# An output stage that loads the first experts and gathers the first blocks before it ends

## What is computed

```
x  = x + g1 * (concat(gla, attn) @ w_out)
h2 = modulate(rms_norm(x), shift2, scale2)
scores = sigmoid(h2 @ router_w); top 4 of 8 groups, top 8 of 64 experts; weights normed * 2.5
routed = sum over the 8: w_e * (silu(h2 @ wg[e]) * (h2 @ wu[e])) @ wd[e]      (FF = 128)
shared = (silu(h2 @ swg) * (h2 @ swu)) @ swd                                  (FF = 256)
y  = rms_norm(x + g2 * (routed + shared))
```

## Time and profile before

| | us |
|---|---|
| median of 3 runs (lowest, highest) | 1642.26 (1637.18, 1643.11) |
| profiled execution, device time | 1637.02 |
| its span, first to last instruction | 1635.2 |
| PE busy | 1496.2 (91%) |
| DVE busy | 722.9 (44%) |
| POOL busy | 564.6 (35%) |
| ACT busy | 530.4 (32%) |
| mean granted PE clock | 0.956 |

### The profile page before, as it was taken

How to read it: one execution, slowest core, us unless ns; L and a number is a source line. 1 busy time by engine, 2 the same in 40 slices (tenths; PEclk the granted TensorE clock), 3 DMA queues, 4 the chain that set the end, 5 groups by cost and what they waited for, 6 DMA issues and landing times. The chain is left out here.

```text
span 1635.2 us, 28990 instructions
## 1 busy us (share of the span) xinstructions
PE 1496.2 (91%) x9223; PEld 922.0 (56%) x9224; DVE 722.9 (44%) x1453; ACT 530.4 (32%) x1255; POOL 564.6 (35%) x615
## 2 busy tenths in 40 slices
PE   5999999999899999999999599999999999999645
PEld 2654678787757774555465255555455555555312
DVE  2300144442455652787843244444344444444238
ACT  2400165443156651211100133333333333333212
POOL 0001134344253211111254255555455555444322
PEclk8999999999989999999999799999999999999868
DMA  9991002100183017012000699999999999986487
GB/s 340 343 341 39 20 2 52 47 14 17 64 305 131 27 63 297 26 52 90 1 0 0 240 315 335 337 331 339 345 342 328 336 295 303 274 206 120 64 314 286
DMA packets 108677, 301.66 MB, mean 184 GB/s; under 512 B 13020, under 2 KB 24112, under 8 KB 107836
## 3 DMA queue, kind: packets, MB, share of 16 engines
q1 hardware_dynamic: 81390, 212.09, 34.5%
q0 software_dynamic: 25920, 83.91, 21.3%
q10 hardware_dynamic: 1296, 4.72, 0.7%
HBM read 230.26 MB, written 80.90 MB: 190 GB/s over the span
## 5 line engine op out<-in xcount | busy, mean ns | idle before, releaser
L2103 PE MATMUL ps_g<-w_exp,mix 128*64 x1408 | 327.4, 386 | 5.8 <-DVE own_gu L2198 2.8
L2106 PE MATMUL ps_g<-own_gu,mix 128*64 128x256 f32 x1408 | 327.4, 386 | 0.0
L2103 PEld LDWEIGHTS ps_g<-w_exp,mix 128*64 128x64 f32 x1408 | 187.7, 138 | 108.2 <-issue 11.9
L2052 POOL DMA_INDIRECT sum_rows<-mix,scatter_row x66 | 128.6, 1948 | 173.1 <-DVE mix L2141 147.1
L2106 PEld LDWEIGHTS ps_g<-own_gu,mix 128*64 128x64 f32 x1408 | 187.7, 138 | 0.0
L2075 PE MATMUL ps_y<-w_exp,hidT 128*64 x352 | 171.6, 610 | 6.3 <-ACT own_d L2154 6.3
L2076 PE MATMUL ps_y<-own_d,hidT 128*64 128x512 f32 x352 | 171.6, 610 | 0.0
L511 PE MATMUL ps_f<-late,hT 128*128 128x256 f32 x624 | 144.9, 389 | 0.0
L2198 DVE COPY own_gu<-w_exp 128x2048 f32 x89 | 109.5, 1231 | 59.2 <-issue 46.4
L511 PEld LDWEIGHTS ps_f<-late,hT 128*128 128x128 f32 x624 | 119.9, 195 | 18.7 <-issue 1.9
L1480 PE MATMUL ps_o<-wo,mixT 128*128 128x512 f32 x288 | 126.0, 596 | 0.5 <-DVE h L1726 0.5
(11 more groups left out here) (328 smaller groups left out, 2497.6 us busy)
## 6 DMA issues: line engine op xcount, KB each, us to landing
w_exp<-in_exp_w_gate SPq DMA_DIRECT2D x64, 512.0 KB, 7.6
w_exp<-in_exp_w_up SPq DMA_DIRECT2D x64, 512.0 KB, 14.6
w_exp<-in_exp_w_down SPq DMA_DIRECT2D x64, 512.0 KB, 21.4
sum_rows<-mix SPq DMA_DIRECT2D x10, 2048.0 KB, 18.4
sums<-sum_rows SPq DMA_DIRECT2D x36, 512.0 KB, 15.1
ada_ring<-in_w_ada SPq DMA_DIRECT2D x8, 2048.0 KB, 11.1
wring<-in_w_ada SPq DMA_DIRECT2D x3, 2048.0 KB, 13.1
h_rows<-h SPq DMA_DIRECT2D x9, 512.0 KB, 2.6
```

The costliest lines, as they stand in the source:

```text
L2052: pool.indirect_dma_start(out=dram["y"][k % 2], out_offset=bass.IndirectOffsetOnAxis(ap=si[k][:], axis=0), in_=y[k], in_offset=None, bound ...
L2103: pe.matmul(ps_g[par][0:HALF, 0:2 * FF].rearrange("p (k f) -> p k f", k=2), xT[par][:, j * P:j * P + HALF], w[:, bass.ds(slot * 3, 2), ff] ...
L2106: last = pe.matmul(ps_g[par][HALF:P, 0:2 * FF].rearrange("p (k f) -> p k f", k=2), xT[par][:, j * P + HALF:(j + 1) * P], own_gu[par][:, :, ...
```

## The change

- `w_exp` (the ring of eight slots) is allocated around both stages. In the output stage its first 36 KB are `h2T` (slots of experts 0 to 2), and `w_out`, the rows of modulation and one of the two `mixT` tiles lie behind it.
- When all of `gate_up` is done (`h2T` is read for the last time) SP loads experts 0, 1 and 2 and waits for them at the stage's end.
- POOL, after the table is written, gathers blocks 0, 1 and 2 into the last three rows of `keep["mix"]` (the x and y buffers change places), then makes the addition of tile 7 and waits for the gathers.
- `down(8)` writes `ps_h` instead of `ps_o`, so it waits for `eb_kept` (block experts copied out of that bank) and no longer for `keep_shared(7)`. DVE makes the last tile's addition to `x1` itself.
- `write_table` copies the gates last instead of first.
- `experts` issues expert 3 at once, posts experts 0 to 2 as ready without a wait, issues 4 to 6 after blocks 0 to 2 are multiplied (`gu_done` 1 to 3), and gathers block 3 first. Before it issued 3 to 6 after `gu_done` 1 to 4.

```diff
@@ -1337,11 +1339,14 @@
             return nc.alloc_semaphore(name)
         GE = 8
-        wo = sb("wo", [P, KD, D])
+        wf = keep["w"][:].rearrange("p s n -> p (s n)")
+        wof = wf[:, KD * T:KD * (T + D)]
+        wo = wof.rearrange("p (j n) -> p j n", n=D)
         rw = sb("rw", [P, KD, NE])
-        mixT = [sb(f"mixT{i}", [P, KD, P]) for i in range(2)]
+        mixT = [wf[:, KD * (T + D) + 6 * D:].rearrange("p (j t) -> p j t", t=P), sb("mixT1", [P, KD, P])[:]]
         g2rows = keep["g2"]
-        rows = sb("rows", [P, 3, 2, D])
+        rof = wf[:, KD * (T + D):KD * (T + D) + 6 * D]
+        rows = rof.rearrange("p (w c n) -> p w c n", w=3, c=2)
         h2 = [sb(f"h2_{i}", [P, D]) for i in range(2)]
         ssq = sb("ssq2", [P, NT])
         lnm = sb("lnm2", [P, NT])
...
@@ -1385,14 +1389,13 @@
         pairs = sb("r_pairs", [1, NE], I32)
         lastf = sb("r_lastf", [1, 3])
-        wof = wo[:].rearrange("p j n -> p (j n)")
         place = [wof[:, i * 1024:(i + 1) * 1024].rearrange("p (k r) -> p k r", r=P) for i in range(2)]
         entry = [wof[:, 2048 + i * 2048:2048 + i * 2048 + 2 * TOPK * TAB].rearrange("p (k v b) -> p k v b", v=2, b=TAB) for i in range(2)]
         empty = wof[:, 6144:6144 + TAB]
         s_sh, h_sh, hT_sh = ([wof[:, 6400 + (2 * k + i) * FS:6400 + (2 * k + i + 1) * FS] for i in range(2)] for k in range(3))
         wgu = keep["mix"][:, 0:2 * KD * FS].rearrange("p (k n) -> p k n", k=2)
         wd = keep["mix"][:, 2 * KD * FS:2 * KD * FS + 2 * D].rearrange("p (k n) -> p k n", k=2)
-        t6 = [mixT[i][:].rearrange("p j n -> p (j n)") for i in range(2)]
+        t6 = [mixT[i].rearrange("p j n -> p (j n)") for i in range(2)]
         ps_t = ps("ps_t4", [P, 2, 512])
         ps_o = ps("ps_o4", [P, 2, 512])
...
@@ -1454,8 +1464,13 @@
                     sp.dma_start(wgu[:, 0, :], dram["sh_w_gate"].rearrange("(p j) f -> p (j f)", j=KD)).then_inc(wgu_in, 16)
                     sp.dma_start(wgu[:, 1, :], dram["sh_w_up"].rearrange("(p j) f -> p (j f)", j=KD)).then_inc(wgu_in, 16)
                     sp.dma_start(wd, dram["sh_w_down"].rearrange("(k p) n -> p k n", p=P)).then_inc(wd_in, 16)
+            sp.wait_ge(gu_done, NT)
+            for e in range(W_EARLY):
+                for k, w in enumerate(expert_weights(dram)):
+                    sp.dma_start(keep["w"][:, 3 * e + k, :], w[e, :, :]).then_inc(first_w, 16)
             sp.wait_ge(h2_out[0], 16 * 5)
             sp.wait_ge(h2_out[1], 16 * 4)
+            sp.wait_ge(first_w, 48 * W_EARLY)
         @block.tensor
         def _(pe):
...
@@ -1532,12 +1547,14 @@
                 if t == 0:
                     pe.wait_ge(wd_in, 16)
                     pe.wait_ge(gx_done, NT)
+                elif t < NT - 1:
+
+                    pe.wait_ge(t_done, t)
                 else:
-
-                    pe.wait_ge(t_done, t)
+                    pe.wait_ge(eb_kept, 1)
                 for q in range(2):
                     for k in range(2):
-                        last = pe.matmul(ps_o[:, q, :], hT_sh[t % 2][:, k * P:(k + 1) * P],
+                        last = pe.matmul(down_bank(t)[:, q, :], hT_sh[t % 2][:, k * P:(k + 1) * P],
                                          wd[:, k, q * 512:(q + 1) * 512], start=(k == 0), stop=(k == 1))
                 last.then_inc(down_done, 1)
...
@@ -1680,6 +1697,13 @@
                 pool.tensor_tensor(v[:, :, 0, :], v[:, :, 0, :], tokp1[:, t:t + 1].unsqueeze(2).to_broadcast([P, TOPK, TAB]),
                                    ALU.mult).then_inc(entry_done, 1)
+            def gather(k):
+                pool.tensor_copy(keep["gi"][k][:], keep["tab"][:, k, 0:1]).then_inc(gi_made, 1)
+                pool.wait_ge(gi_made, k + 1)
+                pool.indirect_dma_start(out=keep["mix"][:, (6 + k) * D:(7 + k) * D], out_offset=None, in_=dram["h2"],
+                                        in_offset=bass.IndirectOffsetOnAxis(ap=keep["gi"][k][:], axis=0),
+                                        bounds_check=T - 1, oob_is_err=False).then_inc(first_x, 16)
+
             def add_shared(t):
                 pool.wait_ge(t_done, t + 1)
                 pool.tensor_tensor(keep["x1"][:, t, :], keep["x1"][:, t, :], t6[t % 2], ALU.add).then_inc(x_done, 1)
...
@@ -1694,8 +1718,15 @@
                 if t % 2:
                     add_shared(t // 2 + 1)
             entries(NT - 1)
-            for t in range(NT // 2 + 1, NT):
-                add_shared(t)
+            add_shared(NT - 4)
+            add_shared(NT - 3)
+            pool.wait_ge(tab_written, 1)
+            pool.wait_ge(h2_out[0], 16 * 5)
+            pool.wait_ge(h2_out[1], 16 * 4)
+            for k in range(X_EARLY):
+                gather(k)
+            add_shared(NT - 2)
+            pool.wait_ge(first_x, 16 * X_EARLY)
         @block.vector
         def _(dve):
...
@@ -1797,7 +1828,7 @@
                     dve.wait_ge(rows_in[3], 16)
                 if t >= 2:
                     dve.wait_ge(x_done, t - 1)
-                dve.tensor_tensor(t6[t % 2], ps_o[:].rearrange("p n k -> p (n k)"), keep["g2"][:, cond_of(t), :], ALU.mult).then_inc(t_done, 1)
+                dve.tensor_tensor(t6[t % 2], down_bank(t)[:].rearrange("p n k -> p (n k)"), keep["g2"][:, cond_of(t), :], ALU.mult).then_inc(t_done, 1)
             def slots():
...
@@ -1849,18 +1880,18 @@
             def keep_block_experts():
                 dve.wait_ge(eb_turned, 1)
-                dve.tensor_copy(keep["bexp"][:].rearrange("o (p c) -> o c p", c=2), ps_e)
+                dve.tensor_copy(keep["bexp"][:].rearrange("o (p c) -> o c p", c=2), ps_e).then_inc(eb_kept, 1)
             def write_table():
                 tab = keep["tab"]
                 dve.wait_ge(tab_done, NT)
                 token = ps_tab[:, 0, :]
-                dve.tensor_copy(tab[:, :, 2].bitcast(F32), ps_tab[:, 1, :])
                 step(dve.tensor_scalar(empty, token, 0.0, float(NOWHERE), ALU.is_equal, ALU.mult))
                 step(dve.scalar_tensor_tensor(out=tab[:, :, 0], in0=empty, scalar=-1.0, in1=token, op0=ALU.add, op1=ALU.add))
                 step(dve.tensor_scalar(empty, token, 0.0, spare, ALU.is_equal, ALU.mult))
                 step(dve.scalar_tensor_tensor(out=tab[:, :, 1], in0=empty, scalar=shift, in1=token, op0=ALU.add, op1=ALU.add))
+                dve.tensor_copy(tab[:, :, 2].bitcast(F32), ps_tab[:, 1, :]).then_inc(tab_written, 1)
             mix_half(0)
             for t in range(NT):
...
@@ -1899,6 +1930,15 @@
             write_table()
             keep_shared(NT - 2)
             keep_shared(NT - 1)
+            dve.wait_ge(t_done, NT)
+            dve.tensor_tensor(keep["x1"][:, NT - 1, :], keep["x1"][:, NT - 1, :], t6[(NT - 1) % 2], ALU.add)
+
+
+def expert_weights(dram):
+
+    return (dram["exp_w_gate"].rearrange("(e p j) f -> e p (j f)", p=P, j=KD),
+            dram["exp_w_up"].rearrange("(e p j) f -> e p (j f)", p=P, j=KD),
+            dram["exp_w_down"].rearrange("(e p) n -> e p n", p=P))
 def experts(nc, dram, keep):
...
@@ -1918,15 +1958,14 @@
         def sem(name):
             return nc.alloc_semaphore(name)
-        NW = 8
         AHEAD = 4
         FOURS = NBMAX // 4
-        w = sb("w_exp", [P, NW * 3, D])
+        w = keep["w"]
         buf = keep["mix"]
-        x = [buf[:, i * D:(i + 1) * D] for i in range(4)]
+        y = [buf[:, i * D:(i + 1) * D] for i in range(4)]
         xT = [buf[:, (4 + i) * D:(5 + i) * D] for i in range(2)]
-        y = [buf[:, (6 + i) * D:(7 + i) * D] for i in range(3)] + [sb("y5_3", [P, D])[:]]
-        gi = [sb(f"gather_row{i}", [P, 1], I32) for i in range(4)]
+        x = [buf[:, (6 + i) * D:(7 + i) * D] for i in range(3)] + [sb("x5_3", [P, D])[:]]
+        gi = keep["gi"]
         si = [sb(f"scatter_row{i}", [P, 1], I32) for i in range(4)]
         s = [sb(f"silu{i}", [P, FF]) for i in range(2)]
         h = [sb(f"hid{i}", [P, FF]) for i in range(2)]
...
@@ -1976,12 +2011,15 @@
         @block.sync
         def _(sp):
             def issue(e, slot):
-                for k, src in enumerate((wg, wu, wd)):
+                for k, src in enumerate(expert_weights(dram)):
                     sp.dma_start(w[:, 3 * slot + k, :], src[e, :, :]).then_inc(w_in[slot], 16)
             def ready(o, i):
-                sp.wait_ge(w_in[i], (o + 1) * 48)
+                if i >= W_EARLY:
+                    sp.wait_ge(w_in[i], (o + 1) * 48)
+                elif not (first(o) and o == 0):
+                    sp.wait_ge(w_in[i], o * 48)
                 sp.sem_inc(w_ready, 1)
             def replace(o, i, wait=True):
...
@@ -1991,16 +2029,12 @@
                     sp.wait_ge(down_done, last)
                 issue(o * NW + (i + NW - 1), (i + NW - 1) % NW)
-            issue(0, 0)
-            issue(1, 1)
-
-            sp.wait_ge(x_in[0], 16)
-            ready(0, 0)
-            issue(2, 2)
-            ready(0, 1)
-            for e in range(3, NW - 1):
-
-                sp.wait_ge(gu_done, e - 2)
```

(36 more changed lines are left out.)

## The result

The changed kernel takes 1623.88 us (median of 4 runs, 1623.31 to 1625.38), the kernel before in the same comparison 1639.99 us (1637.18 to 1643.11). The ratio is 0.9915 with a 95% interval of 0.9898 to 0.9931: about 0.85% faster, 14 us of 1640. The forecast was 1627.5 in a range of 1620 to 1637. The profiled execution took 1623.55 (span 1621.7) against 1637.02 (span 1635.2): 13.5 us less, where the sum said 14.8.

The account below looks back on a forecast made before the run. PE was taken to set the expert stage's pace, weight stream close behind, with holes at the stage boundary and block 33. Stage end 1.1, gather wait 9.7 and late load 4.0 sum to 14.8 us: 1642.3 to 1627.5, range 1620 to 1637.

Parts of the forecast that it names:

- Early loads: Output stage: nine weight loads leave at 889.7 us, land at 903 to 905, hidden behind PE's last products.
- Early gathers: Output stage: three gathers from 898.0 us, the third issued at 903.9 and landed at 907.5, bounds 907.5 and 912.2.
- The last two tiles: End of output stage: product 8 ends at 903.4, DVE's addition at 905.9; both edits worth nothing by themselves.
- The start of the expert stage: Stage boundary: first instruction 1.1 us earlier, 9.7 of the gather wait gone, transposes 10.8 earlier, 4.72 behind them stays.
- Rival 3: Stage boundary: a gather sharing rings with weights ends the stage, PE stays cold longer; gain 4.2, at most 1638.1; chance 0.10.
- The clock: PE's clock at the boundary: same cold stretch, effect 0; bounds 2.7 us better to 1.9 us worse.
- The late load: Expert 29's load at block 33: loss falls from 7.0 us to 3.0, gain 4.0, bounds 0 and 7.0.
- Rivals 1: Block 33: the late load stays as late in PE's time, the queue as full as before; 1631.5 us; chance 0.20.
- 2 (wholly gone): Block 33: the late load's 7.0 us loss goes wholly; 1624.5 us; chance 0.08.
- rival 4: Block 33: the stream has no lead, the stall grows by what PE gains; 1642 us; chance 0.08.
- Rival 5: Output stage: 288 products (126.0 us) read slower from the ring's room; a tenth costs 12.6 us; chance 0.04.
- The sum: Whole kernel: 1.1 + 9.7 + 4.0 = 14.8 us gained, 1642.3 to 1627.5.

Follow-up runs that it names:

- e2: The changed kernel with the three early gathers but no expert loaded before the expert stage: 1633.22 us.
- e6: The changed kernel with the last tile as before (product 8 into ps_o, its addition on GpSimd): 1624.15 us.
- e1: The changed kernel with three experts loaded early and all gathers left to the expert stage: 1630.41 us.
- e8: The changed kernel run again, nothing altered: 1623.07 us.
- e10: The changed kernel run again on another chip, nothing altered: 1623.37 us.
- e3: The changed kernel with experts 3 to 6 issued one block later, after gu_done 1 to 4 as in the kernel before: 1629.08 us.
- e5: The changed kernel with experts 4 to 6 issued at the expert stage's start, without waiting for blocks 0 to 2: 1625.37 us.
- e4: The changed kernel with one early gather instead of three, blocks 1 to 3 gathered at the expert stage's start: 1620.07 us.
- e7: The changed kernel with one early gather and two early experts, experts 2 and 3 issued at the expert stage's start: 1622.46 us.
- e9: The changed kernel with one early gather instead of three, run again on another chip: 1619.90 us.

## Why the prediction was right, by its steps

- **Early loads**: right in place and time (889.84), and hidden.
- **Early gathers**: issue times right to 0.2 us (903.7 for 903.9). The landing was mis-sized: I took 3.6 us for the third and it was 5.2, 1.4 us later in all (908.9 for 907.5). The wait behind the weights that the bound of 8.3 stood for isn't the reason: with no load in flight it was 5.4 (e2).
- **The last two tiles**: "worth nothing by themselves" is right (e6). But DVE's addition, taken at 1.22 with the bound 2.34, took 3.41, over both: I gave both ends for each engine alone and not for the two at once, and set a rule for DVE's copies against this addition, not the one for two inputs in SBUF (last section). It hid under the landing and cost nothing here.
- **The start of the expert stage**: 1.1 us earlier was wrong, it is 0.9 later. This is the step that failed, by 2.0 us: 1.4 for the late landing, and 0.6 for the way from there to the first instruction, 1.8 us where 1.2 was taken from a stage that ended with an addition. The 9.7 us of the gather's wait went entirely (e1 brings 3.9 back with the gathers in the next stage), and the 4.7 behind the transposes stayed (4.79). Rival 3 was right that a gather's landing ends the stage, with 2 us and not 4.7, but e2 doesn't bear out its reason, rings shared with the weights.
- **The clock**: taken as 0, was 1.0 us worse in this profile and 0.4 to 0.5 better in e8 and e10, the same kernel (fourth copy 16.3, 14.8 and 14.9 us after the first product, 15.3 before). Both are within the bounds, whose better end is 2.9 by its own working (half of 1.97 + 3.8), not 2.7.
- **The late load**: 7.0 to 2.3, gain 4.7 where 4.0 was taken, by the mechanism forecast: slots pace loads 13 to 15, the queue behind them is empty (e3, e5). It spreads over experts 29 to 32 as described. The size is in part luck. Load 18 was to leave 10.2 us after load 15 with a lead of 6.5 in PE's time that the stream then keeps; it left 13.6 after, with 3.6, and the lead grew to 7.8 by load 29, while SP ran out of free slots again: behind load 15, up to 1135 us, it waited six times, 15.7 us in all, and not once in the kernel before. Rivals 1 (hole unchanged), 2 (wholly gone) and 4 (hole grows) fall; e2 shows what rival 4 looks like when the weights really have no lead.
- **Rival 5** (slower products out of the ring's room) falls: 125.9 us for 126.0.
- **The sum**: 8.8 - 1.0 + 4.7 = 12.5, and the span lost 13.5; the last 1.0 is in smaller differences after block 38 and at the end that no run isolates. The medians lie 16.1 apart, for the kernel before spreads over 6 us and the changed one over 2. The measured 1623.88 is 3.6 below the 1627.5 forecast; 2.3 of that is the base, 1642.3 where the comparison's own median is 1639.99.

## What to carry to other kernels

A stage that opens with a transfer should have had that transfer in flight before its barrier, but only the first one: what else the barrier waits for ends the stage before, here by 3.3 us. A weight ring's head start pays far from where it is made, in the first stretch where loads are slower than compute, and only as far as free slots let it live until then: look at where the issuing queue waits for slots, and whether anything is in flight there. When an addition is moved to an idle engine, see what its neighbour runs in the same microsecond.

## What the runs showed of the hardware beyond that

- An fp32 addition of 128x1024 within SBUF takes 1.22 us on DVE alone (e1, e4, e7, e9) and 3.40 to 3.43 us when it starts within 0.1 us of one on GpSimd of the same size (changed kernel, e2, e3, e5, e8, e10), which itself keeps its 2.35 us. GpSimd's started first each time, by 0.01 to 0.04 us, and DVE's ends 1.1 us after it, as if it had waited. The Trainium skill, SBUF — State Buffer, section "SBUF: two separate sides", says that a DVE operation with two SBUF inputs and a GpSimd one that reads SBUF exclude each other: the one that starts first has the shared ports for its whole length, the other waits. The traces agree, with GpSimd first.
- A gather's issue was not lengthened by DVE's eviction from PSUM beside it (1.03 us for the third, 903.69 to 904.72). Beside DVE's copies of 128x2048 within SBUF, in the expert stage, it was: 1.38 us beside one copy (changed kernel, e8, e10) and 2.31 us beside two in a row (e9), each time ending 0.12 to 0.13 us after the last copy. The early gathers met no such copy.
- Traces differ before the boundary in how long PE's clock stays low: its mean share from 610 to 620 us is 0.69 to 0.85 in e1, e4, e7 and e9 and 0.91 to 1.00 in the other eight traces, and from 760 to 785 us 0.80 in e1, e4 and e9 and 0.86 in the others. These are the four kernels that reach tile 7's product late; why, no run shows.
